# DeltaNet: shared norms at the end of a head group, and coupling products of four chunks first between substitution and recurrence

## What is computed

```python
def body(s, xs):
    qc, kc, vc, gch, bc = xs
    gc = jnp.cumsum(gch, axis=-1)
    decay = jnp.exp(jnp.where(causal, gc[..., :, None] - gc[..., None, :], -jnp.inf))
    kb = kc * bc[..., None]
    a = jnp.where(strict, jnp.einsum("bhid,bhjd->bhij", kb, kc) * decay, 0.0)
    t = lax.linalg.triangular_solve(a + eye, jnp.broadcast_to(eye, a.shape), left_side=True, lower=True, unit_diagonal=True)
    u = t @ (vc * bc[..., None])
    w = t @ (kb * jnp.exp(gc)[..., None])
    v_new = u - w @ s
    attn = jnp.einsum("bhid,bhjd->bhij", qc, kc) * decay
    o = (qc * jnp.exp(gc)[..., None]) @ s + attn @ v_new
    s = s * jnp.exp(gc[..., -1])[..., None, None] + jnp.einsum("bhcd,bhce->bhde", kc * jnp.exp(gc[..., -1:] - gc)[..., None], v_new)
    return s, o
...
o_dn = rms_norm(o_dn, dn_norm).reshape(bsz, n, DN_VW) * jax.nn.silu(z_dn)
```

## Time and profile before

| | us |
|---|---|
| median of three runs (2818.45 to 2818.95) | 2818.7 |
| the profiled execution, by the device's time | 2821.06 |
| span of its first to last instruction | 2819.3 |
| group 0: keys, substitution | 510.3 to 535.3, to 566.2 |
| group 0: joint, recurrence, end | to 595.3, to 651.8, to 665.7 |
| group 1: the same five | 670 to 695.2, 726.1, 755.1, 811.6, 825.5 |

### The profile page before, as it was taken

The page is one execution under the profiler, slowest core; times in us unless marked ns, Lnnn a source line. Parts: engine busy times, 40 slices in busy tenths (PEclk is TensorE's granted clock), DMA queues, the critical chain, the costliest instruction groups (busy, mean ns, idle before and its releaser), DMA issues.

```text
span 2819.3 us, 41171 instructions
## 1 busy us (share of the span) xinstructions
PE 2616.6 (93%) x15734; PEld 2194.4 (78%) x15734; DVE 1408.0 (50%) x2164; ACT 1094.1 (39%) x1903; POOL 863.0 (31%) x388
## 2 busy tenths in 40 slices
PE   7999999777679899999999998999889998899999
PEld 5888888665665688888888886889678886888887
DVE  4988874565757832344334348632657662311111
ACT  4444432546366532321221225442656665322221
POOL 2222222534436512223222222222200006344443
PEclk9999999888789999999999998999999998999999
DMA  7344454103020131233332323323785502222222
GB/s 280 115 141 134 134 185 167 68 24 123 24 90 1 53 120 51 99 119 105 119 133 92 112 83 107 129 101 106 228 245 135 147 30 75 75 90 91 103 90 90
DMA packets 124112, 311.16 MB, mean 110 GB/s; under 512 B 11712, under 2 KB 38848, under 8 KB 122560
## 3 DMA queue, kind: packets, MB, share of 16 engines
q1 hardware_dynamic: 101936, 262.51, 28.2%
q10 hardware_dynamic: 22032, 46.67, 4.7%
HBM read 253.30 MB, written 55.84 MB: 110 GB/s over the span
## 4 chain that ended last, share of the span: by engine, by line
PE 71%; DVE 13%; issue 7%; ACT 5%; DMA 1%; POOL 1%; ACTq 1%; SPq 0%; DVEq 0%; POOLq 0%
PE ps L536 16%; PE ps L537 16%; PE ps L538 16%; DVE ybuf L2446 4%; PE ps L1290 4%; PE ps L1314 3%; PE ps L1300 2%; PE ps L1034 1%; PE ps L1236 1%; DVE ps L2516 1%; DVE Vall L2520 1%; PE ps L1215 1%; DVE nmd L2328 1%; DVE ps L2358 1%; PE ps L1216 1%
## 5 line engine op out<-in xcount | busy, mean ns | idle before, releaser
L515 POOL TENSOR_TENSOR Wl<-raws,Wh 128x2048 fp32r<-128x2048 f32 (+3 forms) x138 | 598.7, 4338 | 1644.4 <-ACT Wh L509 1644.4
L536 PE MATMUL ps<-Hh,Wh 128*128 128x512 f32 (+1 forms) x1792 | 622.1, 347 | 18.1 <-ACT ubuf L1526 10.9
L537 PE MATMUL ps<-Hl,Wh 128*128 128x512 f32 (+1 forms) x1792 | 614.5, 343 | 0.0
L538 PE MATMUL ps<-Hh,Wl 128*128 128x512 f32 (+1 forms) x1792 | 608.6, 340 | 0.0
L536 PEld LDWEIGHTS ps<-Hh,Wh 128*128 128x128 f32 x1792 | 339.8, 190 | 69.4 <-ACT ubuf L1526 12.6
L537 PEld LDWEIGHTS ps<-Hl,Wh 128*128 128x128 f32 x1792 | 339.4, 189 | 40.9 <-issue 3.1
L538 PEld LDWEIGHTS ps<-Hh,Wl 128*128 128x128 f32 x1792 | 338.0, 189 | 42.4
L509 ACT ACTIVATE Wh<-raws 128x2048 fp32r<-128x2048 f32 (+3 forms) x140 | 247.4, 1767 | 238.8 <-PE ps L538 199.1
L2834 DVE TENSOR_TENSOR hdb<-sgb,ps 128x768 f32<-128x768 f32 (+1 forms) x44 | 36.1, 821 | 364.3 <-PE ps L538 364.3
L2757 DVE SCALAR_TENSOR_TENSOR xT<-ps,mod,xT 128x512 f32 (+1 forms) x82 | 52.2, 663 | 311.0 <-PE ps L538 310.6
L2446 DVE SCALAR_TENSOR_TENSOR ybuf<-ubuf,vec,ybuf 128x770 f32<-128x770 f32 x144 | 184.4, 1280 | 42.4 <-ACT ybuf L1532 27.5
(11 more groups left out here) (390 smaller groups left out, 5164.4 us busy)
## 6 DMA issues: line engine op xcount, KB each, us to landing
raws<-in_slabs SPq DMA_DIRECT2D x234, 512.0 KB, 4.3
adl<-in_ada ACTq DMA_DIRECT2D x48, 512.0 KB, 3.9
ada<-in_ada SPq DMA_DIRECT2D x32, 512.0 KB, 4.4
chunks<-obuf ACTq DMA_DIRECT2D x52, 256.0 KB, 3.3
ada<-in_ada SPq DMA_DIRECT2D x8, 1024.0 KB, 5.0
chunks<-obuf ACTq DMA_DIRECT2D x52, 128.0 KB, 3.2
chunks<-uh SPq DMA_DIRECT2D x17, 384.0 KB, 2.5
lows<-ul SPq DMA_DIRECT2D x17, 384.0 KB, 2.7
```

What stands on the lines that cost most here:

```text
L515: nc.gpsimd.tensor_tensor(Wl[n % 2][:, 0:w], raw[n % 2][:, 0:w], Wh[n % 2][:, 0:w].bitcast(f32), ALU.subtract).then_inc(sig("slab_lo"), 1)
L536: nc.tensor.matmul(o, lhs(c)[0], rhs(c, t0, t1)[0], start=(s == 0), stop=False)
L537: nc.tensor.matmul(o, lhs(c)[0], rhs(c, t0, t1)[1], start=False, stop=False)
L538: last = nc.tensor.matmul(o, lhs(c)[1], rhs(c, t0, t1)[0], start=False, stop=(s == k - 1))
```

## The change

All of it is inside DeltaNet, and runs in both groups.

1. Keys: VectorE copies two of the four diagonal blocks of every chunk, right after the chunk's product; ScalarE keeps two. The diagonal of `Vall` is written by ScalarE. ScalarE takes the first chunk's query products before that, and squares the queries in two parts between the first chunks. `kcol` is turned after `bsc`.
2. Joint: TensorE issues `couple` of four chunks first, then far, far, couple, corner, far, couple, and corner and far in turn. VectorE copies the `R6` blocks first with a signal of their own (`dn_yy`), and then the `TTs` blocks. Of the four blocks 32x768, VectorE copies two after the fourth chunk, ScalarE two after the first `far`.
3. End: the third and fourth chunk of `FINAL` change places. Their sums (ScalarE) are made before the last step's work. Of the last two, the sums move to VectorE (four instructions with accumulators each, then an addition of `ksm`, which holds the scaled bias). The bias of the other two is added by GpSimd, so that ScalarE needs one logarithm of 128x4 per chunk. The scaling is GpSimd's for the third and fourth chunk, ScalarE's for the fifth, VectorE's for the last.

The diff without the counters' numbering:

```diff
 SV = 132
-FINAL = ((4, 1, 1), (5, 1, 0), (1, 4, 1), (2, 4, 0), (3, 5, 0), (0, 5, 1))
...
 
-                pe.wait_ge(sig("dn_ye5"), 6 * g + q + 1)
...
                 pe.wait_ge(sig("dn_xe6"), 6 * g + q + 1)
...
-            pe.wait_ge(sig("dn_w"), past("dn_w") + 2 * g + 2)
+            pe.wait_ge(sig("dn_w"), past("dn_w") + 3 * g + 3)
             pe.wait_ge(sig("dn_kv"), 12 * g + 12)
-            for s in range(NT + 2):
...
+            for q in range(4):
+                couple(q, INTRA[q])
+            pe.wait_ge(sig("dn_r6"), past("dn_r6") + g + 1)
+            far(0, INTRA[0])
+            far(1, INTRA[1])
+            couple(4, INTRA[4])
+            pe.wait_ge(sig("dn_tx1"), past("dn_tx1") + 2 * g + 2)
+            corner(0, INTRA[0])
+            far(2, INTRA[2])
+            couple(5, INTRA[5])
+            for q in range(1, 4):
+                corner(q, INTRA[q])
+                far(q + 2, INTRA[q + 2])
+            corner(4, INTRA[4])
+            corner(5, INTRA[5])
...
-                for a in range(4):
+                for a in range(2):
...
+            taken(0, INTRA[0])
+            act.wait_ge(sig("dn_sv"), past("dn_sv") + SV * g + 5)
+            act.wait_ge(sig("dn_z"), past("dn_z") + 4 * g + 2)
+            nc.scalar.activation(Vall[:, :, :, :].rearrange("p d i n -> p d (i n)")[:, :, 0:BS * BS:BS + 1], bsc[:, :, :], ACT.Copy)\
+                .then_inc(sig("dn_sv"), 1)
...
+            act.wait_ge(sig("ld_dq"), 16 * g + 16)
+            for x in range(2):
+                nc.scalar.activation(dsq[:, 2 * x:2 * x + 2, :].rearrange("p h t -> p (h t)"),
+                                     dq[:, 2 * x:2 * x + 2, :].rearrange("p h t -> p (h t)"), ACT.Square).then_inc(sig("dn_sq"), 1)
+                if x == 0:
+                    taken(1, INTRA[1])
+                    scaled_values(INTRA[1])
+            for q in range(2, NT):
+                taken(q, INTRA[q])
...
+            far_taken(0)
+            for a in (2, 3):
+                ins = nc.scalar.activation(TTs[block32(a), :, 1, :, block32(a)],
+                                           WTc[1][block32(a), :, 0:24].rearrange("p n (c h) -> p c h n", c=NT), ACT.Copy)
+            ins.then_inc(sig("dn_tx1"), 1)
+            far_taken(1)
+            for q, c in enumerate(INTRA):
+                corner_taken(q, c)
+                if q + 2 < NT:
+                    far_taken(q + 2)
...
+                if f < 2:
+                    act.wait_ge(sig("dn_osum"), 6 * g + f + 1)
+                    act.wait_ge(sig("dn_qe"), 2 * g + 1)
+                    for h in range(4):
+                        ins = nc.scalar.activation(osum[:, c, h:h + 1], osum[:, c, h:h + 1], ACT.Ln, scale=1.0 / P,
+                                                   bias=qcol[:, 4 * c + h:4 * c + h + 1])
+                    ins.then_inc(sig("dn_oln"), 1)
+                else:
+                    act.wait_ge(sig("dn_oq"), past("dn_oq") + 4 * g + f - 1)
+                    nc.scalar.activation(osum[:, c, :], osum[:, c, :], ACT.Ln, scale=1.0 / P).then_inc(sig("dn_oln"), 1)
...
+                if f == 4:
+                    act.wait_ge(sig("dn_on"), 6 * g + 4)
...
+                if k == NT - 1:
+                    summed(2)
+                    summed(3)
...
-                if k == NT - 1:
-                    summed(2)
-                    summed(3)
-                    rooted(2)
-                    rooted(3)
-                    scaled(2)
-                    scaled(3)
-            for f in (4, 5):
-                summed(f)
+            for f in range(2, NT):
                 rooted(f)
+                if f == 4:
+                    scaled(f)
...
+            for f in (2, 3):
+                c = FINAL[f][0]
+                pool.wait_ge(sig("dn_osum"), 6 * g + f + 1)
+                pool.wait_ge(sig("dn_qe"), 2 * g + 2)
+                nc.gpsimd.tensor_tensor(osum[:, c, :], osum[:, c, :], ksm[:, 4 * c:4 * c + 4], ALU.add)\
+                    .then_inc(sig("dn_oq"), 1)
+            for f in (2, 3):
+                c = FINAL[f][0]
+                pool.wait_ge(sig("dn_orec"), 6 * g + f + 1)
+                if f == 2:
+                    pool.wait_ge(sig("dn_on"), 6 * g + 2)
+                nc.gpsimd.tensor_tensor(oacc[:, c, :, :], oacc[:, c, :, :], orst[:, c, :].unsqueeze(2).broadcast_to([P, 4, P]), ALU.mult)\
+                    .then_inc(sig("dn_on"), 1)
...
+                dve.wait_ge(sig("dn_ke"), 6 * g + q + 1)
+                for a in (2, 3):
+                    ins = nc.vector.tensor_copy(KEc[block32(a), :, 4 * c:4 * c + 4].rearrange("p i s -> p s i"),
+                                                KE[block32(a), c, :, block32(a)])
+                ins.then_inc(sig("dn_kc"), 1)
...
-            nc.vector.transpose(kcol[:, :], ksm[:, :]).then_inc(sig("dn_ks"), 1)
             dve.wait_ge(sig("dn_sv"), sv + 4)
...
                 .then_inc(sig("dn_sv"), 1)
+            nc.vector.transpose(kcol[:, :], ksm[:, :]).then_inc(sig("dn_ks"), 1)
...
-            dve.wait_ge(sig("dn_z"), past("dn_z") + 4 * g + 2)
-            nc.vector.tensor_copy(Vall[:, :, :, :].rearrange("p d i n -> p d (i n)")[:, :, 0:BS * BS:BS + 1], bsc[:, :, :]).then_inc(sig("dn_sv"), 1)
...
+            dve.wait_ge(sig("dn_z"), past("dn_z") + 4 * g + 4)
...
+                yt, y = (ps[:, b + q % 2, 0:128].rearrange("p (h n) -> p h n", h=4) for b in (6, 4))
+                nc.vector.tensor_copy(R6[block32(1), 4 * c:4 * c + 4, 0:BS], y[block32(1), :, :])
+                nc.vector.tensor_copy(R6[block32(2), 4 * c:4 * c + 4, BS:64], y[block32(2), :, :]).then_inc(sig("dn_yy"), 1)
                 dve.wait_ge(sig("dn_tx0"), past("dn_tx0") + 6 * g + q + 1)
...
                 for a in range(4):
...
+                    ins = nc.vector.tensor_copy(TTs[block32(a), c, a % 2, :, block32(a ^ 1)], yt[block32(a), :, :])
+                ins.then_inc(sig("dn_ye5"), 1)
+                if q == 3:
+                    for a in (0, 1):
                         ins = nc.vector.tensor_copy(TTs[block32(a), :, 1, :, block32(a)],
                                                     WTc[1][block32(a), :, 0:24].rearrange("p n (c h) -> p c h n", c=NT))
                     ins.then_inc(sig("dn_tx1"), 1)
...
+            dve.wait_ge(sig("dn_oq"), past("dn_oq") + 4 * g + 2)
+            for f in (4, 5):
+                c, k, d = FINAL[f]
+                dve.wait_ge(sig("rec_o"), 12 * g + 2 * k + d + 1)
+                for h in range(4):
+                    ins = nc.vector.scalar_tensor_tensor(xjunk[:, f % 2, h, :], oacc[:, c, h, :], 1.0, oacc[:, c, h, :], ALU.mult, ALU.mult,
+                                                         accum_out=osum[:, c, h:h + 1])
+                ins.then_inc(sig("dn_osum"), 1)
+                dve.wait_ge(sig("dn_osum"), 6 * g + f + 1)
+                nc.vector.tensor_tensor(osum[:, c, :], osum[:, c, :], ksm[:, 4 * c:4 * c + 4], ALU.add)\
+                    .then_inc(sig("dn_oq"), 1)
...
+            c = FINAL[5][0]
+            dve.wait_ge(sig("dn_orec"), 6 * g + 6)
+            dve.wait_ge(sig("dn_on"), 6 * g + 5)
+            nc.vector.tensor_tensor(oacc[:, c, :, :], oacc[:, c, :, :], orst[:, c, :].unsqueeze(2).broadcast_to([P, 4, P]), ALU.mult)\
+                .then_inc(sig("dn_on"), 1)
```

106 lines of the change are left out of this document (39 added, 67 removed).

## The result

The changed kernel takes 2800.74 us in the median of four runs (2797.46 to 2803.83), beside 2818.57 for the kernel before: a ratio of 0.9937 with a 95% interval of 0.9925 to 0.995, or 17.8 us less (14 to 21). The forecast was 2808 with a range of 2799 to 2814. The execution profiled took 2802.94 us for a span of 2801.1. The direction and the range held; the gain is 7 us larger than forecast, and the part of it that was missed lies in three places that the stretches show.

The account below looks back on a forecast made before the run. TensorE, busy 93%, but waiting at the changed places on ScalarE or VectorE. Per group keys -0.3, joint -1.2, end -3.8 make -5.3, for both -10.6: 2810.5 for the profiled execution, 2808 for the median, range 2799 to 2814.

Parts of the forecast that it names:

- rival 1: Group ends: TensorE's clock stays up, so the next stage starts at full speed; -17.2 us, 2801.5, chance 0.22.
- Rival 2: Keys: VectorE and GpSimd collide less, gaining 1.6 to 2.8 us there; 2804.5 in total, chance 0.13.
- rivals 3 and 4: Third: new owners of moved work become the bound, 2812, chance 0.12; fourth: joint's clock rises late, 2822, chance 0.05.
- Keys, -0.3 forecast: Keys, per group: of 2.8 us gross gain, collisions of GpSimd's products with VectorE leave 0.3.
- one engine behind the other: Keys: GpSimd's 3.8 us and VectorE's 2.4 and 0.2 run serially from 528.6; substitution starts at 535.0, against 535.28.
- The range's other end: Keys: VectorE's new copies cannot get in between GpSimd's eight masks, with GpSimd's work ahead elsewhere too; +2.0 us.
- Joint, -1.0 and -1.4 forecast: Joint, first and second group: first corner 0.8 us later in the first, less copying behind it; mean -1.2.
- I let it rise 3.5 to 4 us after: Joint: TensorE's clock rises that long after the first corner at 585.25, giving about 9.1 us to the recurrence.
- End, -3.8 forecast: End, per group: sums and scalings leave ScalarE, so the last gate product ends at 661.85 instead of 665.70.
- I take 0.38 each: End: assumed time of each VectorE square sum for the fifth chunk, 1.5 us for its sums, plus 0.2 for the addition.
- The bound of -5.2: End, per group: largest gain allowed, with VectorE's sums at 0.26 us and TensorE at the full clock.
- Rival 4: Joint and recurrence: clock rises late, costing +2.4 and +3.2 us; +3 in all, 2822, chance 0.05.

Follow-up runs that it names:

- gp_late: Changed kernel plus one wait: GpSimd's first three products wait for VectorE's two Bs and ScalarE's Vall; 2801.16 us, ratio 0.9934 to the kernel before.
- joint_alone: Kernel before with only the edits to the joint between substitution and recurrence; 2816.22 us, ratio 0.9989 to the kernel before.
- fill_end: gp_late plus 21 small unread TensorE products per group in the gaps at its end, nine behind the last turn; 2801.68 us, ratio 0.9938 to before.
- fill_end2: As fill_end, on gp_late, but three instead of nine unread products behind the last turn; 2796.09 us, ratio 0.9914 to the kernel before.
- sums_back: Changed kernel with the last two chunks' square sums and roots back on ScalarE; 2806.46 us, ratio 0.9951 to the kernel before.
- scale_back: Changed kernel with the scalings of chunks three and four back on ScalarE; 2801.77 us, ratio 0.9937 to the kernel before.

## Why the prediction was right, and where it missed

- **The number.** The measured 2800.74 lies within the range, but 7 us from the forecast and next to rival 1's 2801.5, though rival 1 did not happen. Rival 2 did not either (its sign was -1 or more in the keys), nor rivals 3 and 4. The mechanisms of the forecast held, and the sizes below were off, all to the same side.
- **Keys, -0.3 forecast, -0.53 measured in group 0.** The sum (one engine behind the other from the first query product on, 6.4 us) had GpSimd's start to within 0.1 (527.39, 18.3 us after the first product, as 528.6 was) and the order of the collision. It missed 0.2: behind each of GpSimd's products the waiting instruction of VectorE ended a little sooner than one that starts afresh (1.09 after GpSimd's third product for the first `Bs`, usually 1.23). gp_late shows that the collision is what takes the gain: 2.2 us come back without it, so that of 2.8 gross 2.7 are reached. The range's other end (copies held by the masks) was not reached; the copies of group 0 were held for up to 1.2 us a pair, and no chunk's keys came later.
- **Joint, -1.0 and -1.4 forecast, -1.3 and -2.3 in the profiled run.** The first corner came where the sum had it, in both groups. The step "I let it rise 3.5 to 4 us after" the first corner held in this run (3.6 and 3.4), and not in joint_alone, gp_late, fill_end, fill_end2 and sums_back in group 0 (5.4 to 6.3), nor in joint_alone, gp_late and fill_end2 in group 1 (6.2, 6.4 and 4.4). Over the seven profiles with this joint and no filling in it the mean is 28.5 and 27.35, against 29.0 for three with the old one: -0.5 and -1.6 or -2.2 together, where the forecast has -2.4. The size was right on average and the reason right, but that the clock rose so early in this run was luck: no row of before could place it, nor TensorE's standstill.
- **End, -3.8 forecast, -5.5 measured.** The mechanism and the order of every step are as forecast. The term that was mis-sized is VectorE's sum: "the nearest is 0.34, 0.26 from start to start, with 0.14 for the accumulator. I take 0.38 each". It is 0.21 from start to start, so eight sums and two additions take 2.0 instead of 3.4. That is 1.4 of the 1.65 by which the end from the last `to` on is shorter, 8.35 instead of 10.0; GpSimd is done 0.1 earlier and the gates and the last scaling take 0.2 less. The bound of -5.2 (0.26 each, full clock) was too narrow for the same reason, and the low clock at the end did come. The scalings on GpSimd were counted as part of the gain; scale_back shows that they are none.
- **Clock at the ends.** Rival 1 had it staying up, with -2.9 in the next stage. It fell, and the next stage still began at half speed: the products of group 1 took 3.65 and not 1.88. But it came back after 3.4 us instead of 5.8, which the forecast, with "3.0 us in all" taken as fixed, did not allow for: 1.2 us. Rival 4's price has a reading of its own that is off: "some 6.4 us at half speed before it rises, as after 667.44" is 5.8 there, so +2.9 and not +3.2.
- **The sum.** Ends 2 x 1.7 more, group 1's keys 1.3 more, the joints 1.2 more in this execution, group 0's keys 0.2: that is the whole 6.2 between -10.6 and -16.8; 1.3 us more had been gained ahead of group 0, where nothing was changed, so chance. The clock's part of it, 1.2 in group 1's keys and most of the joints' 1.2, was not foreseen either and is luck of the same kind.
- **No slower case.** Recurrence and substitution are unchanged to 0.02 us, and the clock was up before the recurrence in every profile.

## What to carry to other kernels

Before an elementwise product of GpSimd is moved forward, look which VectorE instructions with two SBUF inputs it will stand beside; here a wait of one line on GpSimd, which had 7.9 us to spare later, gave 2.2 us in the keys of group 0, and still nothing in the median (2801.16 against 2800.74). A gain of a microsecond ahead of a stretch at the low clock need not arrive behind it: look at the granted clock of that stretch in several kernels before crediting or blaming an edit, and try small products in TensorE's gaps, counted so that they end before the next product could start. When work is shared out over three engines, take each share back once: one of them may be worth nothing.
